# Window mask added in PSUM, softmax division moved to the read-out, and the second norm of the mixture block applied token by token, with its router products inside the merge

## The reference, cut to what matters

```python
for l in range(2):
    hx = rms_norm(x, norm1_g[l]) * (1.0 + sc1) + sh1
    y = token_mixers(hx, hc, ...)            # gating, Fourier, two attentions, then @ w_out
    x = x + g1 * y
    h = rms_norm(x, norm2_g[l]) * (1.0 + sc2) + sh2
    x = x + g2 * expert_choice_ffn(h, router_w[l], wg, wu, wd)

# differential attention: two softmax maps of each head
    a = softmax(s);  w = a[:, :, 0] - lam * a[:, :, 1];  y = w @ v
# neighbourhood attention: a bias table, and -inf outside the window
    s_loc = where(valid, q @ k * scale + bias, -inf)
# expert choice, 16 experts with 32 tokens each
    aff = softmax(h @ router_w)              # (tokens, 16)
    gate, idx = top_k(aff.T, 32);  xg = h[idx]
    o = (silu(xg @ wg) * (xg @ wu)) @ wd * gate
```

## Time and profile before

| | |
|---|---|
| median of 3 runs | 2525.82 us (2521.6 to 2529.7) |
| profiled execution: time, span | 2531.14 us, 2529.4 us |
| PE busy | 2276.5 us (90% of the span) |
| DVE busy | 1146.3 us (45%) |
| ACT busy | 860.0 us (34%) |
| POOL busy | 67.7 us (3%) |
| chain that ended last | PE 62%, DMA 27%, DVE 6%, ACT 3% |

### The profile page before, as it was taken

One profiled execution on the slowest core, in us unless ns is written; L12 is line 12 of the kernel. 1 busy time (PEld: TensorE's weight loads), 2 busy tenths in 40 slices (PEclk: granted clock), 3 DMA queues, 4 the chain that ended last, 5 costly groups with the idle time before them and its releaser, 6 DMA issues.

```text
span 2529.4 us, 28645 instructions
## 1 busy us (share of the span) xinstructions
PE 2276.5 (90%) x12121; PEld 1482.1 (59%) x12121; DVE 1146.3 (45%) x1654; ACT 860.0 (34%) x1212; POOL 67.7 (3%) x99
## 2 busy tenths in 40 slices
PE   6998899888887898898888778999999999999997
PEld 3865653234232585732222215889898888877887
DVE  4545441012010655420001005758877577658766
ACT  4435421001000434410000004544755465535544
POOL 0022000000000002000000000000000000000000
PEclk9999999999999998999999999999999999999999
DMA  6374368999999440369999997445354454462442
GB/s 283 117 295 202 131 266 347 428 427 429 427 428 428 188 170 39 134 278 427 428 428 427 429 428 302 175 171 217 113 221 176 167 195 176 159 239 100 188 162 105
DMA packets 63567, 660.62 MB, mean 261 GB/s; under 512 B 7152, under 2 KB 8688, under 8 KB 19664
## 3 DMA queue, kind: packets, MB, share of 16 engines
q1 hardware_dynamic: 62336, 653.68, 63.3%
q0 software_dynamic: 1104, 5.11, 0.6%
HBM read 657.71 MB, written 1.05 MB: 260 GB/s over the span
## 4 chain that ended last, share of the span: by engine, by line
PE 62%; DMA 27%; DVE 6%; ACT 3%; issue 1%; SPq 0%; POOL 0%; DVEq 0%; ACTq 0%; POOLq 0%
DMA ring<-in_exp_up 19%; PE ps L754 19%; PE ps L755 10%; PE ps L1113 7%; DMA ring<-in_exp_down 6%; PE ps L726 4%; PE ps L727 4%; PE ps L728 4%; PE ps L1137 3%; PE ps L777 1%; PE ps L893 1%; DMA ring<-in_ada_w 1%; PE ps L1234 1%; PE ps L1087 1%; PE ps L916 1%
## 5 line engine op out<-in xcount | busy, mean ns | idle before, releaser
L1113 PE MATMUL ps<-ring,arena 128*64 128x512 f32 (+1 forms) x2048 | 461.7, 597 | 106.0 <-DMA ring<-in_exp_up 56.3
L754 PE MATMUL ps<-h_buf_r,ring_r 128*128 128x512 f32 x1408 | 501.4, 401 | 6.6 <-DVE h_buf_r L619 6.6
L384 DVE TENSOR_TENSOR ring_r<-ring,ring_r 128x2048 fp32r<-128x2048 f32 (+4 forms) x198 | 417.1, 2133 | 196.7 <-ACT ring_r L376 195.5
L755 PE MATMUL ps<-h_buf_r,ring_r 128*128 128x256 f32 x1408 | 396.7, 282 | 0.0
L1113 PEld LDWEIGHTS ps<-ring,arena 128*64 128x64 f32 (+1 forms) x2048 | 126.3, 123 | 436.9 <-issue 253.5
L376 ACT ACTIVATE ring_r<-ring 128x2048 fp32r<-128x2048 f32 (+4 forms) x198 | 346.9, 1782 | 73.9 <-DMA ring<-in_ffn_w 51.8
L754 PEld LDWEIGHTS ps<-h_buf_r,ring_r 128*128 128x128 f32 x1408 | 266.0, 189 | 73.4 <-issue 7.5
L755 PEld LDWEIGHTS ps<-h_buf_r,ring_r 128*128 128x128 f32 x1408 | 267.4, 190 | 0.1
L2159 DVE TENSOR_TENSOR h_buf<-h_buf,ps 128x512 f32<-128x512 f32 (+1 forms) x32 | 21.9, 683 | 514.0 <-PE ps L1113 514.0
L1137 PE MATMUL ps<-ring,h_buf 128*64 128x512 f32 (+1 forms) x1024 | 230.1, 596 | 26.8 <-ACT h_buf L1570 18.9
L754 PE MATMUL ps<-arena_r,ring_r 128*128 128x512 f32 x660 | 233.4, 399 | 0.0
(11 more groups left out here) (292 smaller groups left out, 3013.8 us busy)
## 6 DMA issues: line engine op xcount, KB each, us to landing
ring<-in_exp_gate SPq DMA_DIRECT2D x64, 2048.0 KB, 25.6
ring<-in_exp_up SPq DMA_DIRECT2D x64, 2048.0 KB, 25.6
ring<-in_exp_down SPq DMA_DIRECT2D x64, 2048.0 KB, 24.7
ring<-in_ffn_w SPq DMA_DIRECT2D x88, 1024.0 KB, 6.8
ring<-in_ada_w SPq DMA_DIRECT2D x24, 2048.0 KB, 12.8
ring<-in_ffn_w SPq DMA_DIRECT2D x64, 704.0 KB, 5.4
ring<-in_w_in SPq DMA_DIRECT2D x6, 2048.0 KB, 16.0
ring<-in_w_out SPq DMA_DIRECT2D x4, 2048.0 KB, 7.7
```

The costliest lines, as they stand in the source:

```text
L384: dve.tensor_tensor(rest, slot(n)[:, at], lead, ALU.subtract).then_inc(sem("chunk_halved"), 1)
L754: release(pe.matmul(ps[:, bank, :], w[0][:, lo:lo + P], both, start=start, stop=False, skip_group_check=True))
L755: return pe.matmul(ps[:, bank, 0:N], w[1][:, lo:lo + P], both[:, 0:N], start=False, stop=stop, skip_group_check=True)
L1113: mm = pe.matmul(ps[half * m:half * m + m, which, :], xe[:, k, :], slot(c)[:, at:at + 512], start=k == 0, stop=k == KT - 1)
```

## The change

1. Mask: GpSimd no longer adds it to the bias table. Once, in layer 0, ahead of `c_bands`, it copies the identity and the mask to bf16; each of the eight units of `attention_d` in a layer that have a window adds the mask by one more bf16 product of 256 columns.
2. Division: `weights` forms e0 + e1 * (-lam * sum0 / sum1) in one pass over both maps; `read_out` divides by sum0, by a reciprocal of four columns and a product with it in place of the copy.
3. Second norm: VectorE writes `scaled_x = x * gain` behind each `mix_added`, and sums the squares. TensorE multiplies each tile by the router weights one step later in the merge (`token_logits`: one product for each 128 tokens, activations stationary, 16 columns moving). The mean is taken by token in one column; the factor `tok_rstd` is applied to the logits and at the reads of the turned activations. The shift goes to the logits through `shift_logits` (16 products in layer 0, 8 in layer 1, ahead of the merge), and to the gathered tokens in `pick`.
4. Order of `route`: six (layer 1: four) blocks are turned without a wait between; `ada_products(5)` comes behind the turned affinities; the first gather is split by stream; most `stay_busy` of layer 0 and some of layer 1 are gone.

```diff
@@ GpSimd
+                if l == 0:
+                    pool.tensor_copy(ident_b[:, :], ident)
+                    pool.wait_ge(sem("att_loaded"), 16)
+                    pool.tensor_copy(mask_b[:, :], att[:, columns(ATT, "mask")]).then_inc(sem("mask_ready"), 1)
...
-                pool.tensor_tensor(biases, biases, masks, ALU.add).then_inc(sem("bias_ready"), 1)
@@ TensorE, attention_d scores, q < 2
-                        mm = pe.matmul(ps[:, u % 3, 0:N], ident, rel_bias[:, q, h, :], start=False, stop=True)
+                        pe.matmul(ps[:, u % 3, 0:N], ident, rel_bias[:, q, h, :], start=False, stop=False)
+                        mm = pe.matmul(ps[:, u % 3, 0:N], ident_b[:, :], mask_b[:, :], start=False, stop=True)
@@ TensorE, merge
-                stay_busy(0, 13)
+                shift_logits(l)
+                stay_busy(0, 2 if l == 0 else 7)
...
+                    if d:
+                        token_logits(l, d - 1)
+            def token_logits(l, k):
+                tiles = 4 if l == 0 else 2
+                pe.wait_ge(sem("mix_scaled"), k + 1 + before("mix_scaled", l))
+                for t in range(tiles):
+                    mm = pe.matmul(ps[:, 0, EXPERTS * t:EXPERTS * t + EXPERTS], scaled_x(k)[:, P * t:P * t + P],
+                                   router_sb[:, l, k, :], ...)
+            def token_means(l):
+                pe.wait_ge(sem("mix_squares_added"), l + 1)
+                pe.wait_ge(sem("norm_squares"), KT * i + KT)
+                for t in range(4 if l == 0 else 2):
+                    own, out = slice(P * t, P * t + P), ps[:, 7, 64 + t:65 + t]
+                    release(pe.matmul(out, squares(i)[:, 0, own], mean_w[:, 0:1], start=True, stop=False))
+                    mm = pe.matmul(out, squares(i)[:, KT - 1, own], mean_w[:, 0:1], start=False, stop=True)
@@ TensorE, route
+                token_means(l)
+                token_logits(l, KT - 1)
+                pe.wait_ge(sem("mix_added"), KT + before("mix_added", l))
+                for j in range(turned_first(l)):
+                    turn_tokens(l, j)
+                if l:
+                    stay_busy(3, 4)
                 pe.wait_ge(sem("aff"), 1 + before("aff", l))
...
-                stay_busy(5, 34 if l == 0 else 24)
+                if l == 0:
+                    ada_products(5)
+                    ada_turn(5)
+                if l:
+                    stay_busy(3, 24)
                 pe.wait_ge(sem("slots"), 1 + before("slots", l))
@@ TensorE, gather_half
+                    if half == 0 and b == 4:
+                        for j in (6, 7):
+                            pe.wait_ge(sem("h_tok_rest"), j - 2 + before("h_tok_rest", l))
+                            turn_tokens(l, j)
+                    if half == 0 and pair == 0:
+                        pe.wait_ge(sem("gather_ready"), s + 1 + before("gather_ready", l))
+                        pe.wait_ge(sem("h_tok_rest"), 4 * s + 4 + before("h_tok_rest", l))
@@ TensorE, main
-                norm_pe(pe, release, 2 * l + 1)
-                if l == 0:
-                    ada_products(5)
-                else:
-                    stay_busy(5, 12)
@@ ScalarE, route and pick
+                act.wait_ge(sem("norm_mean"), 2 * l + 2)
+                act.activation(tok_rstd[:, 0:tiles], ps[:, 7, 64:64 + tiles], ACT.Sqrt, ...)
+                act.activation(exp_table, eps_col[:, 0:1], ACT.Exp)
...
-                    act.activation(*picked_bank(l, b), ACT.Copy).then_inc(sem("picked_act"), 1)
+                    for k in range(2):
+                        ins = act.activation(out[:, k, :, :], own[:, k, :, :], ACT.Identity, bias=col)
@@ VectorE, attention_c
-                dve.tensor_copy(ycat[:, q, 2 * GROUP:3 * GROUP], ps[:, 7, 0:GROUP]).then_inc(sem("c_out"), 1)
+                link(dve.reciprocal(den, den))
+                dve.tensor_tensor(y, out, bc(den, HEAD), ALU.mult).then_inc(sem("c_out"), 1)
...
-                link(dve.tensor_scalar(e1, e1, den[:, 1:2], None, ALU.mult))
-                dve.scalar_tensor_tensor(e0, e0, den[:, 0:1], e1, ALU.mult, ALU.add).then_inc(sem("c_weights"), 1)
+                dve.scalar_tensor_tensor(e0, e1, den[:, 1:2], e0, ALU.mult, ALU.add).then_inc(sem("c_weights"), 1)
```

More of the change, by code:

```diff
@@ L688, in norm_tile @@
         def norm_tile(eng, i, k):
[L690 to L695, removed]
+            eng.wait_ge(sem("norm_halved"), KT * sum(in_halves(j) for j in range(i)) + k + 1)
         SC = GROUP // P
@@ L733, in stay_busy @@
             def stay_busy(bank, times):
+                one = zeros[:, :]
+                four = bass.AP(one.tensor, one.offset, [list(one.ap[0]), [0, 4], list(one.ap[1])])
                 for _ in range(times):
-                    pe.matmul(ps[:, bank, :], zeros[:, 0:P], zeros[:, :], start=True, stop=True, skip_group_check=True)
+                    pe.matmul(ps[:, bank, :], one, four, start=True, stop=True, skip_group_check=True)
             def h_tile(k):
@@ L1001, in route @@
                 rows_ = 48 if l == 0 else 16
[L1003 to L1018, removed]
-                            mm = pe.transpose(ps[:, 0, EXPERTS * t:EXPERTS * t + EXPERTS],
-                                              logits_t[0:EXPERTS, P * t:P * t + P], ident[0:EXPERTS, 0:EXPERTS])
-                        mm.then_inc(sem("logits_turned"), 1)
-                if l == 0:
-                    ada_turn(5)
-                stay_busy(5, 4 if l == 0 else 9)
+                token_means(l)
[5 more added lines that the diff above has]
+                    stay_busy(3, 4)
                 pe.wait_ge(sem("aff"), 1 + before("aff", l))
@@ L2078, in route @@
[L2078 to L2085 removed]
+                    dve.scalar_tensor_tensor(h_tok_rest[half][:, t, :], ps[:, bank, :], tok_rstd[:, t:t + 1],
+                                             h_tok[:, t, 512 * half:512 * half + 512], ALU.mult, ALU.subtract)\
+                        .then_inc(sem("h_tok_rest"), 1)
@@ L2120, in route, with pick @@
                         .then_inc(sem("spread_rows"), 1)
-                pick(l, 0)
-            def pick(l, half):
+            def pick(l, half, todo):
                 banks = 8 if l == 0 else 4
-                for b in range(1, banks, 2):
+                for b in todo:
                     dve.wait_ge(sem("gathered"), banks * half + b + 1 + before("gathered", l))
-                    dve.tensor_copy(*picked_bank(l, b)).then_inc(sem("picked_dve"), 1)
+                    out, own = picked_bank(l, b)
+                    shift = mod[:, l, 3 * KT + 2 * (b % 4):3 * KT + 2 * (b % 4) + 2, b // 4]
+                    dve.tensor_tensor(out, own, bc(bc(shift, 8), CAP), ALU.add).then_inc(sem("picked_dve"), 1)
             def spread_out(l, s):
```

197 lines of the change are left out of this document (127 added, 70 removed).

## The result

The changed kernel took 2502.2 us (median of 4 runs, 2498.8 to 2507.6) against 2525.9 before: ratio 0.9907, 95% interval 0.989 to 0.9924, 23.7 us less. The forecast was 2503. A later measurement of the same code, the control of the last experiments, gave 2507.5 us and 0.9917 (0.9899 to 0.9935). The profiled execution took 2504.4, with a span of 2502.6 against 2529.4.

What follows compares the result with a forecast made beforehand. The experts' DMA weight stream was taken as the bound, so time saved on the chain from attention_c to experts counts: -6.2 - 5.0 + 1.0 - 8.3 - 4.6 + 0.5 = -22.6, giving 2503 us; 8 in 10: 2490 to 2514.

Steps and rivals of the forecast that it cites:

- 10.5 against 5.1: Layer 0's attention_c: the stalled unit and next two take 5.1 us instead of 10.5 without the mask add, -5.4.
- 1.00 through its last units: Sign in the changed profile: TensorE's clock at 1.00 through the last units of layer 0's attention_c.
- The tail behind it I leave as it is: the wait that precedes it stays: Layer 1's attention_c: the tail (984 to 996, clock 0.50) stays unchanged, beside a forecast -5.0 us.
- more: Rival: layer 1's half-clock stretch (984 to 996) goes too, giving some 7 us; 2492 to 2497; chance 0.15.
- 0.105 us a pass, 5.9 and 2.9: Merge: narrow router passes cost 0.105 us each whatever the columns, +5.9 us in layer 0, +2.9 in layer 1.
- the clock's +3.0, bounds 0 and +6: Layer 0, merge to experts: lower clock costs transposes 1.2 and the modulation's products 1.8 us; +3.0, bounds 0 and +6.
- at the same low clock: Layer 1, from the gather to the experts: 6.4 us as now, with the clock as low as before.
- the 0.8 for the idle products: Layer 1, merge to experts: +0.8 us for a lower clock in the 24 idle products, ending behind the slots.
- Slower: Rival: each merge switch between wide fp32r and narrow fp32 products exposes the whole latency, 0.46 us a pass; chance 0.03.
- doesn't arrive: Rival: freed time is waited off at the DMA as last expert chunks land late; 2511, or 2518 and over; 0.06.
- the 0.2 us a pass: Merge: narrow router products cost 0.2 us a pass, +8 us, 2511; in the lesser-gain rival, chance 0.20.
- The narrow work holds the clock down: Rival, less gain: half clock lasts through ada_products(5) (+5.2), gathers (+3) and merge starts (+3); 2514; chance 0.20.

Runs made afterwards that it cites:

- e1: Kernel before with only the mask moved into bf16 products into PSUM; 0.9946 of the kernel before, -13.7 us.
- e4: Changed kernel with each narrow router product inside the two merges issued a second time, into unread columns; 0.9936 of the kernel before, -16.2 us.
- e2: Kernel before with only the division by map 1's sum moved to the read-out, GpSimd's mask add kept; 0.9978 of the kernel before, -5.6 us.
- e11: e9 with layer 1's router products one step later in the merge; 2491.7 us, 0.9862 of the kernel before.
- e7: Changed kernel with wide products on zeros where TensorE waits ahead of a fall of the clock; 0.9864 of the kernel before, -34 us.
- e5: Changed kernel with layer 0's ada_products(5) and its turning put ahead of the affinities' transposes; 0.994 of the kernel before, -15.2 us.
- e9: e7 with more zero products around each merge's last transposes and ahead of layer 0's second gather; 2494.3 us, 0.9877 of the kernel before.
- e6: Changed kernel with all router products taken out of the merge and put behind its last wide product; 0.991 of the kernel before.
- e3: Changed kernel with mask add and division put back as before; 0.9949 of the kernel before, -12.9 us.
- e10: e9 with the router products behind the merge and wide products between them; 2496.8 us, 0.988 of the kernel before.

## Why the prediction was right

The time was right to 1 us, by terms that were off by more and in both directions; that closeness is luck. The control took 2507.5 us with the same code. What was right by its mechanism is the stall, the price of the narrow passes and the shorter strand from the merge to the experts.

- **Mask.** Shown by e1: the stall goes with GpSimd's add alone, and after the whole change the passes come at the interval worked out. What was off is the sum "10.5 against 5.1" as the stage's gain: layer 0 gave 4.5, not 6.2. With the stall and its recovery gone, the fall of the clock comes in the tail (208) and takes back 1.3 us. That a stretch at full clock before stays so wasn't worked out, only the sign "1.00 through its last units" was named; it showed false. The -0.3 in that sum has no reason given.
- **Mask, layer 1.** "The tail behind it I leave as it is: the wait that precedes it stays": 7.3 instead of 5.0, since the tail now stays at 1.00. In e4 it didn't, and the stage gave 4.8. This is the rival "more", in part, and it varies from one execution to the next: the half clock came behind the tail instead (974 to 982).
- **Division.** -0.5 once in each layer and +0.2 back is too small to be told from the traces' spread; beside the mask's part they show 0.15 and 0.07. That it matters little where TensorE is full held. e2's expectation was right in layer 0 and wrong in layer 1.
- **bf16 products.** They take 0.11 us each on the chain, against 0.12 forecast. The stage up to the merge, in which they lie, shows +0.44 and +0.41 against +0.3 and +0.7, but there the traces spread by more (69.3 to 71.3 us in layer 0).
- **The shift products,** put at nothing because they stand in a wait. In layer 0 they took 4.82 us at half clock, where 3.4 was reckoned, and TensorE came to the merge last: 283.21, with VectorE done at 282.37. That is 0.8 us on the path; in the control 1.1, and 2.7 in layer 1, together with the zeros behind them.
- **Merge.** 0.105 us a pass, 5.9 and 2.9: measured 0.80 us for eight, +5.6 and +3.4 for the stage, and doubling them costs about the same again (e4). The row of 64 columns priced a product of 16, so the columns don't matter here; that it is the weight load that sets the price isn't shown. Layer 1's extra 0.5 is the 0.49 us of wait that e11 removes. The 81 ns that the Trainium skill gives ("TensorE: Matmul & The Clock Gate", Back-to-back issue gap) for weight load and product of 128 columns in a stream lie below this trace: 100 ns a pass in layer 0's merge; in layer 1's merge and in e7's shift products, at full clock, four passes take 0.35 us, 88 ns, nearer to it.
- **Merge to experts, layer 0.** -14.2 forecast, -14.6 measured, -11.7 in the control; top-k beside `ada_products(5)` shown by e5. (The prediction's 25.4 is 25.7 by its own terms; its end, 30.3, is right.) Of the clock's +3.0, bounds 0 and +6: the last router piece lost 0.4 (1.23 for 0.80), the turned blocks 1.2 (3.99 for 24, where 24 transposes of that size at the merge's start take 2.84 in e9 at full clock) and some 16 products of the gather 1.5 (0.21 instead of 0.12 each), 3.1 in all. By the same count the control lost 5.5 to 6, at the forecast's bound. The size is right in one trace and a place wrong in both: the modulation's products, for which I had counted 1.8, took 7.05 at full clock as before, and the gather lost it instead.
- **The same, layer 1.** -7.5 forecast, -9.6 measured. I took the gather "at the same low clock"; it ran at 1.00 (1064 to 1068), and the 0.8 for the idle products did not show.
- **The rivals.** "Slower" (0.46 us a pass) and the 0.2 us a pass are out by e4; "doesn't arrive" by the queue's rows. "The narrow work holds the clock down" is true of places (280 to 286, 344 to 348), but each fall was over within 3 to 10 us.

Most of the misses have one cause: I treated the clock as something that a removed wait gives back, and left the rest of its course in place. It moved instead: 52 us at half clock before, 48 after, 51 in the control. e7, with 17, shows what lay in those falls: some 10 us, as far as the zeros caused its gain.

## What to carry to other kernels

Count a removed stall twice: once for itself, once for the clock behind it; then look where the next wait or narrow stretch lies, since the fall can come there. Parts that remove the same stall don't add, so price each with the others in place. Narrow router products kept full clock between wide ones and lost it behind them in layer 0. A wait that the engine sits out is the place for something wide, if traces confirm that the clock stays up. Take more than one trace of the same code before reading 1 to 3 us from a stage.

## What the runs showed of the hardware

- The clock's fall came at different units in executions of the same code: layer 1's `attention_c` took 31.45, 31.15, 31.49, 34.00 and 30.64 us (after, control, e6, e4, e5), and layer 0's stretch from merge to experts 31.46 to 35.81 (after, control, e3, e4). A stage that holds such a place can't be judged from one trace.
- With wide products on zeros the clock was at 1.00 in `attention_c`'s tails (0.65 of about 1.4 us) and in the shift products, in all four kernels that had them. Behind the merge of e10, with two zeros behind each router piece, it was at 1.00 in layer 1 (four passes a piece) and at 0.50 in layer 0 (eight); with eight ahead of the token means it stayed at 1.00 in layer 0 of e7 and fell in that of e9. I can't say from these runs what separates them.
- A VectorE `scalar_tensor_tensor` on a single column, with all its operands in SBUF, took 2.40 us instead of 0.22 beside GpSimd's add, to within 0.02 us of its end (e2). So a step needn't be large to be held. But not every step is: a reciprocal on one column of SBUF, 0.19 us earlier and beside the same add, took its usual 0.15.
- A narrow fp32 pass (16 columns) costs 0.10 us between layer 0's wide products (512 columns), 0.088 between layer 1's (256 columns) and in e7's shift products, all at full clock, and 0.19 to 0.21 at half clock (1.52 us for 8, 6.85 for 32).
